# Issuing all sixteen moves of x's turned tokens from GpSimd

## The reference

```
proj = u @ w_in                         # columns: pooling | z | x, B, C | dt | gates
xbc  = silu(causal_depthwise_conv(xbc, conv_w, conv_b))      # 4 taps along the tokens
xs, Bm, Cm = split(xbc)                 # x: 8 groups of 8 heads of 64 channels
y    = ssd_scan(xs, dt, A, Bm, Cm) + d_skip * xs
y    = rms_norm_per_group(y * silu(z))
```

## Time and profile before

| | |
|---|---|
| median of 3 runs | 2701.09 us (2700.38 to 2704.89) |
| profiled execution | 2700.27 us, span of its instructions 2698.6 us |
| busy: PE, PEld | 2688.8, 2239.4 us |
| busy: DVE, ACT, POOL | 1625.6, 1301.5, 435.2 us |
| granted TensorE clock | 0.999 of full speed over the span |
| loop over the eight groups | about 1147 to 1530 us of the span |

### The profile page before, as it was taken

How to read it: one execution, slowest core, us unless ns; L and a number is a source line. 1 busy time by engine, 2 the same in 40 slices (tenths; PEclk the granted TensorE clock), 3 DMA queues, 4 the chain that set the end, 5 groups by cost and what they waited for, 6 DMA issues and landing times.

```text
span 2698.6 us, 36325 instructions
## 1 busy us (share of the span) xinstructions
PE 2688.8 (100%) x12332; PEld 2239.4 (83%) x12332; DVE 1625.6 (60%) x1899; ACT 1301.5 (48%) x1484; POOL 435.2 (16%) x771
## 2 busy tenths in 40 slices
PE   9999999999999999999999999999999999999998
PEld 8888888888888888888888888888888888888887
DVE  5555555544577555878888865566565555554444
ACT  5444444444455444455565654455654444444443
POOL 1121212000011100132332301232101212120000
PEclk9999999999999999999999999999999999999999
DMA  7776767666566766777677666777557767676664
GB/s 244 205 208 199 209 201 210 195 198 198 175 199 203 231 201 190 200 206 229 200 213 225 201 205 202 210 235 218 175 181 208 207 203 210 200 207 200 198 196 160
DMA packets 324267, 550.28 MB, mean 204 GB/s; under 512 B 62576, under 2 KB 63472, under 8 KB 323920
## 3 DMA queue, kind: packets, MB, share of 16 engines
q1 hardware_dynamic: 263520, 504.00, 62.0%
q0 software_dynamic: 27840, 41.06, 5.6%
q10 hardware_dynamic: 32816, 4.01, 1.0%
HBM read 519.53 MB, written 2.16 MB: 193 GB/s over the span
## 4 chain that ended last, share of the span: by engine, by line
PE 98%; DVE 1%; ACT 0%; ACTq 0%; issue 0%; DVEq 0%
PE J L713 31%; PE J L715 30%; PE J L714 30%; PE J L790 1%; PE J L747 1%; PE J L750 1%; PE J L749 1%; PE A L1022 1%; PE A L1021 1%; PE J L762 0%; PE A L804 0%; PE J L727 0%; PE J L729 0%; PE J L728 0%; DVE wl L1637 0%; PE A L1032 0%
## 5 line engine op out<-in xcount | busy, mean ns | idle before, releaser
L1637 DVE TENSOR_TENSOR wl<-raw,wh 128x1024 fp32r<-128x1024 f32 x950 | 1155.7, 1222 | 937.7 <-ACT wh L1160 929.2
L1160 ACT ACTIVATE wh<-raw 128x1024 fp32r<-128x1024 f32 x950 | 1002.7, 1060 | 1224.7 <-PE J L715 1100.2
L713 PE MATMUL J<-wh,ul 128*128 128x512 f32 x2512 | 980.0, 390 | 0.1
L715 PE MATMUL J<-wl,uh 128*128 128x512 f32 x2512 | 977.6, 389 | 0.0
L714 PE MATMUL J<-wh,uh 128*128 128x512 f32 x2512 | 977.4, 389 | 0.0
L715 PEld LDWEIGHTS J<-wl,uh 128*128 128x128 f32 x2512 | 471.5, 188 | 98.2
L713 PEld LDWEIGHTS J<-wh,ul 128*128 128x128 f32 x2512 | 471.6, 188 | 97.8 <-ACT wh L1160 0.5
L714 PEld LDWEIGHTS J<-wh,uh 128*128 128x128 f32 x2512 | 471.6, 188 | 97.0
L576 POOL DMA_DIRECT2D hraw<-turned x320 | 173.8, 552 | 735.9 <-DVE turned L1821 729.4
L713 PE MATMUL J<-wh,hidl 128*128 128x512 f32 x680 | 264.7, 389 | 0.0
L715 PE MATMUL J<-wl,hidh 128*128 128x512 f32 x680 | 264.5, 389 | 0.0
(11 more groups left out here) (297 smaller groups left out, 1950.0 us busy)
## 6 DMA issues: line engine op xcount, KB each, us to landing
raw<-in_ffn_w_dram SPq DMA_DIRECT2D x528, 512.0 KB, 4.3
raw<-in_w_in_dram SPq DMA_DIRECT2D x257, 512.0 KB, 4.2
raw<-in_w_ssd_out_dram SPq DMA_DIRECT2D x64, 512.0 KB, 3.7
raw<-in_w_pool_out_dram SPq DMA_DIRECT2D x32, 512.0 KB, 4.2
raw<-in_w_mix_out_dram SPq DMA_DIRECT2D x32, 512.0 KB, 5.8
hraw<-turned POOLq DMA_DIRECT2D x320, 32.0 KB, 4.0
csb<-cs_dram POOLq DMA_DIRECT2D x16, 512.0 KB, 7.2
raw<-in_pool_w_dram SPq DMA_DIRECT2D x8, 512.0 KB, 4.6
```

What stands on the lines that cost most here:

```text
L713: nc.tensor.matmul(o[:, t], b, wh[:, r, kk], start=(k == 0 and kk == 0), stop=False)
L715: mm = nc.tensor.matmul(o[:, t], a, wl[:, r, kk], start=False, stop=(k == last_k and kk == CK - 1))
L1160: nc.scalar.activation(wh[:, r], raw[:, r], ACT.Copy).then_inc(high, 1)
L1637: nc.vector.tensor_tensor(wl[:, r], raw[:, r], wh[:, r].bitcast(F32), ALU.subtract).then_inc(low, 1)
```

## The change

The jobs ("x", g) leave `SHARED_MOVES`. POOL then issues all sixteen moves of each x, columns 0 to 3, in one row; ACT issues none of them and goes from its chunk preparation to the exponential of the decays. DVE's convolution of x waits for 256 more of `f_moved` per group where it waited for 128, and no longer for `f_moved_act`. POOL's wait before the last bias rows asks for ACT's moves of C1, the last that it still makes. Pin, C0, B1 and C1 stay shared, B0 stays with POOL. Sizes, source, destination and the order of the other work are the same.

```
--- before.py
+++ after.py
@@ -399,7 +399,7 @@
         CONVS = ["B0", "C0", "B1", "C1", ("x", 0)]
         TURNED_JOBS = ["pin0", "pin1", "pin2", "pin3", "B0", "C0", "B1", "C1"] + [("x", g) for g in range(GROUPS)]
 
-        SHARED_MOVES = ["pin0", "pin1", "pin2", "pin3", "C0", "B1", "C1"] + [("x", g) for g in range(GROUPS)]
+        SHARED_MOVES = ["pin0", "pin1", "pin2", "pin3", "C0", "B1", "C1"]
 
         def f_number(name):
 
@@ -655,7 +655,7 @@
                     pool.wait_ge(conv_done, CONVS.index(("x", 0)) + g + 1)
                     load_csb(g + 1)
             pool.wait_ge(f_moved, pool_moves(("x", GROUPS - 1)))
-            pool.wait_ge(f_moved_act, act_moves(("x", GROUPS - 1)))
+            pool.wait_ge(f_moved_act, act_moves("C1"))
             for j in range(2):
                 load_row(("gate_b", j), b_gate[0:1, D + j * NCOL:D + (j + 1) * NCOL])
             move_y(GROUPS - 1)
@@ -1478,9 +1478,6 @@
                 to(c0 + CD + 1, i, per)
                 if i is None:
                     conv_silu("C1", cT[:], bc_silu)
-                for c in range(M // 2, M):
-                    to(c0 + CD + 1 + c - M // 2, i, per)
-                    move_column(("x", 0), x_in, c, i)
                 to(c0 + CD + 3, i, per)
                 act.wait_ge(seg_ready, lin(1, i, 1))
                 g = slice(0, 1) if i is None else bass.ds(i, 1)
@@ -1922,7 +1919,7 @@
 
                 nb = CONV // P
                 o = x_in if blk_per else b0_in if name == "B0" else bc_in
-                dve.wait_ge(f_moved, lin(pool_moves(name), i, 128))
+                dve.wait_ge(f_moved, lin(pool_moves(name), i, 256 if blk_per else 0))
                 if name in SHARED_MOVES:
                     dve.wait_ge(f_moved_act, lin(act_moves(name), i, 128))
```

## The result

| | before | changed |
|---|---|---|
| median | 2701.08 us (2700.04 to 2704.89, 13 runs) | 2706.54 us (2705.02 to 2707.68, 13 runs) |
| profiled execution | 2700.27 us, span 2698.6 | 2705.21 us, span 2703.5 |

The ratio is 1.0019, 95% interval 1.0012 to 1.0026: 5.1 us slower by the ratio, 5.5 by the medians. Forecast were 2702.1 and a range up to 2705.5. The changed kernel's median lies 1 us above it.

A forecast was written before the change was run, and what follows sets the result against it. PE, busy 2688.8 of 2698.6 us, was taken to bound the kernel. Removed and added work counted 0, late convolutions +1.0 us, giving 2701.3 profiled; 0.8 more to the runs' median gave 2702.1 us, range 2699.5 to 2705.5.

The forecast's parts named there:

- What is removed, worth 0: ACT's 64 x moves, 40.4 us in all, lie off the path; its Copies, paced by PE, stay put: worth 0.
- What is added: POOL's time, y moves, csb: POOL issues 64 more moves at 585 ns, 37.4 us in idle time; y moves 1.8 us later, csb loads unharmed: cost 0.
- When the sixteenth lands: In group 2 POOL's last x move starts at 1254.5 behind a weight load, takes 4.0 us and lands at 1258.5.
- The Trainium skill's rule on queues: DMA engines alternate queues packet by packet, so the sixteenth move would land by 1256.3 and the cost be 0; not adopted.
- What a late convolution costs: +0.15 us per group: On VectorE, a late convolution delays low halves and silu that PE needs: 0.15 us per group, +1.0 us over seven groups.
- Lateness: Delay of the convolution's start on VectorE in group 2: 0.85 us, 0.9 with the step to VectorE.
- Slack: PE's margin before a late low half stalls it: 0.88 us less 0.05 for a semaphore hop, 0.83.
- Group 0, counted 0: In the first group the sixteenth move, issued by 1155.9, has 4.6 us before the convolution at 1160.5: cost 0.
- Nothing seen (0.27): First rival: the sixteenth move lands in time or gets by the weight load; 0 us, 2701.1 us, chance 0.27.
- Slower for good by B0's 6.0 us of latency: Second rival: POOL's moves pile up behind weight loads, convolution 2.9 us late; 14.5 us, 2715.6 us, chance 0.09.
- The trap of the Trainium skill: GpSimd can't write DMA descriptors during VectorE's two-port fp32 instructions; if acting, some tenths of a us per group.
- A gain (at most 0.1 us said): Third rival: relieved ACT or DMA engines bring something forward; at most 0.1 us, 2701.0 us, chance 0.04.

The follow-up runs named there:

- SP's eight: Against the kernel before: POOL keeps eight moves of each x, SP issues the other eight around z's last weight load, ACT none; 2700.75 us, ratio 0.9999.
- the low half put first: Changed kernel, but VectorE makes one weight chunk's low half ahead of the convolution instead of behind its first step; 2701.11 us, ratio 1.0001 against before.
- load held: Changed kernel, but SP holds back the weight load in front of the sixteenth move until the moves have landed; 2702.66 us, ratio 1.0006 against before.
- twenty: Changed kernel with four more DMAs to an unused tensor in front of POOL's sixteen moves; 2730.59 us, ratio 1.0110.
- lateness without relief: Kernel before, ACT keeping its eight moves, with eight extra POOL copies to an unread tensor in front of POOL's own; 2707.20 us, ratio 1.0023.
- fourteen and two: Against the kernel before: POOL issues fourteen moves of each x and ACT the last two; 2700.69 us, ratio 1.0000.
- fifteen and one: Against the kernel before: POOL issues fifteen moves of each x and ACT one; 2702.80 us, ratio 1.0006.

## Why the prediction was wrong, step by step

- *What is removed, worth 0.* Right in its price, wrong in its ground. "ACT's Copies ... stay where they are": they came 2.4 us forward. I had read "[1.71 <-PE J L715]" before the Copy at 1251.06 as a wait for PE that would stay; the DMA issues ahead of it in ACT's program had ended only 0.12 us earlier and were the real hold. From group 1 on PE has no use for it, as the runs with two moves left on ACT and with SP's eight show (ratios 1.0000 and 0.9999).
- *What is added: POOL's time, y moves, csb.* Right: 582 ns each, y moves 2.0 us later (1.8 said), csb still behind the convolution; the low half put first shows that none of it costs.
- *When the sixteenth lands.* Right: behind the weight load, after 3.9 us (4.0 said), 12.7 us after POOL's first move. The load held shows the cause. The Trainium skill's rule on queues (DMA: Bandwidth & Descriptors, section "Queues, rings and completion order"), from which I had concluded that a small move should slip past a load, does not say that: it lets an engine change queues only after a whole packet, which it puts at 9 to 17 descriptors typically. The profile of before counts 263520 pieces for the 504 MB of the queue with the weight loads, about 2 KB each, so by an estimate a load has some 256 of them, 16 on each of the 16 DMA engines, which can be one turn under that rule. My conclusion did not hold: 4.1 us against 1.8.
- *What a late convolution costs: +0.15 us per group.* This step failed: the mechanism was right, and both of its terms were mis-sized. **Lateness** was put at 0.9 us and is 1.31 in group 2: 0.27 us pass from the landing to VectorE's start (0.05 said), the first step takes 0.14 longer in this group, and the move itself is 0.05 later against the convolution's old place. **Slack** was put at 0.83 us and is 0.66. PE starts 0.14 us after a low half, where I took 0.05 for every hop: 0.88 - 0.14 = 0.74. And a chunk whose first matmul had to wait costs a little more by itself: its second matmul follows after 0.31 us, where 0.23 is usual. That takes 0.08 us more, 0.74 - 0.08 = 0.66. So 1.31 - 0.74 + 0.08 = 0.65 us of stall in group 2 in place of 0.1, and from VectorE's turn of x to PE's turn of its convolution the trace has 26.28 us there against 25.63 before. My experiments were planned with the silu as the tighter limit (0.95 - 0.29 = 0.66); the trace does not bear that out, for PE never waited for a silu in the changed kernel, and the hop after one is 0.13 us where it did wait (the load held, group 1). Groups 3 and 7, put at 0 and 0.5 us, lost 0.76 and 0.64; 0.78 is the mean of the six periods from group 1 on.
- *Group 0, counted 0.* Some 0.3 us net: its convolution waited for the moves too. In the five other versions that relieve ACT, twenty left out, the first period is 49.1 to 49.2 us, against 49.7 before and 50.0 in the changed kernel: 0.5 us of gain and 0.8 of loss, neither of them counted.
- *Why so small an error mattered.* Delay and slack nearly cancelled in my sum, 0.9 - 0.83. A difference of two terms of about 1 us, each uncertain by 0.3, times seven, deserved a range of several us, and I closed it at 0.5 us of stall per group.
- *The rivals.* Nothing seen (0.27): refuted. Slower for good by B0's 6.0 us of latency: its point of decision, 0.77 us of stall per group, was reached in the mean (0.78), yet not by its mechanism, for no x move of group 1 to 7 took over 4.3 us. The trap of the Trainium skill (SBUF — State Buffer, section "SBUF: two separate sides"): POOL's issues had a median of 582 ns, the longest 797, so at most 0.2 us of it can be seen in one move. A gain (at most 0.1 us said): 0.5 us in group 0, and none from group 1 on, where PE had no use for it.

Where the time of each execution lies, by the same line of VectorE's turn (first start in group 0 to last start in group 7; before, 1489.3 - 1145.6):

| kernel | seven periods, us | median against before, us |
|---|---|---|
| before | 343.7 | 0 |
| changed | 348.7 | +5.5 |
| lateness without relief | 347.1 | +5.6 |
| fourteen and two | 343.1 | -0.9 |
| fifteen and one | 345.0 | +1.2 |
| SP in place of ACT | 343.2 | -0.9 |
| low half first | 343.5 | +0.2 |
| load held | 343.9 | +1.8 |

A single execution has its own spread, and what group 7 loses comes after the seven periods: 2.5 us in lateness without relief, 0.7 in the load held.

No version beat the kernel before by more than the measurement tells: fourteen and two, SP's eight, and the low half first are all at its level (ratios 1.0000, 0.9999, 1.0001). All sixteen moves can thus stay on GpSimd for nothing, if VectorE uses its wait for one low half.

## What to carry to other kernels

A stall is lateness minus slack, and when both are near 1 us the hops between engines decide: take them from the trace (here 0.14 us from VectorE to PE and 0.27 from a landing to VectorE), not as a small allowance, and keep the range as wide as their sum times the number of rounds. What a small DMA takes depends on whether a large load is in flight beside it, so look at what stands in front of the last of a row of moves. Where PE is close to 100% busy, look for a stall in the distance of its matmuls and in the waits of the engine that feeds it, since PE's busy time and its own table of waits hid nearly all of a loss of 5 us.

## What the runs showed of the hardware beside that

- A 32 KB move between partitions of SBUF on GpSimd's queue landed after 1.8 us with no weight load in front of it and after 3.9 to 4.1 us just behind one of 512 KB, and the last of sixteen landed 0.2 us after that load. Issued 0.17 us ahead of the load it took 3.8 and 4.6 us.
- ACT's DMA issues (0.63 us each) hold back its next computation: eight fewer let its Copies start 2.4 us earlier, while the profile had named PE as what they waited for.
- After waits of 2.2 to 3.1 us on PE its granted clock was at 0.50 for about 3.4 us in four of seven groups, and at 1.00 in the other three; the changed kernel, whose waits on PE stay under 0.4 us in groups 1 to 7, kept 1.00 over the whole loop.
- PE mostly started 0.14 us after the end of the low half that it waited for and 0.13 us after a silu that it waited for; VectorE started 0.27 us after the landing of a move.
